# One MLP block instead of two halves, sample rows in column strips, and smaller mask and scratch tiles in the recurrence

## The reference, cut to what matters

```python
# recurrence, per head (64 x 64 state S), six heads
sa = einsum('nhij,nhj->nhi', S, -kk_t)
S = S * w_t + sa * (kk_t * a_t) + v_t * k_t        # outer products
y_t = einsum('nhij,nhj->nhi', S, r_t)
# afterwards group norm of y per head, bonus term, gate

u = einsum('nld,df->nlf', rmsnorm(x, norm2_g), mlp_up)          # 1024 -> 4096
x = x + einsum('nlf,fd->nld', square(relu(u)), mlp_down)        # 4096 -> 1024
y = rmsnorm(x, final_norm_g)
```

## Time and profile before

| | |
|---|---|
| median of three runs | 3599.7 us (3597.3 to 3603.0) |
| the profiled execution | 3601.9 us |
| its span, first to last instruction | 3600.1 us |
| mean granted TensorE clock | 0.927 |
| TensorE busy in matmuls | 3212.1 us |
| VectorE, ScalarE, GpSimd busy | 1604.0, 828.3, 345.7 us |
| recurrence cp, about | 1046 to 1720 us of the span |
| recurrence cs, about | 1720 to 1830 us |
| MLP half ma, first to last matmul | 2065.6 to 2783.6 us |
| MLP half mb, first to last matmul | 2803.7 to 3592.9 us |

### The profile page before, as it was taken

The page is one execution under the profiler, slowest core; times in us unless marked ns, Lnnn a source line. Parts: engine busy times, 40 slices in busy tenths (PEclk is TensorE's granted clock), DMA queues, the critical chain, the costliest instruction groups (busy, mean ns, idle before and its releaser), DMA issues. The chain is left out here.

```text
span 3600.1 us, 65975 instructions
## 1 busy us (share of the span) xinstructions
PE 3212.1 (89%) x27206; PEld 2722.0 (76%) x27206; DVE 1604.0 (45%) x3139; ACT 828.3 (23%) x1540; POOL 345.7 (10%) x473
## 2 busy tenths in 40 slices
PE   7999998997957788878479789999998799999998
PEld 7999985564646677777458578888887688888887
DVE  6111113764125556554233344444445444444445
ACT  5000002653002222221122221212112222111122
POOL 3000002641002322321000000000000000000000
PEclk9999999998658989999579899999999899999999
DMA  4212213323310000000145531111111411111011
GB/s 148 69 69 70 71 71 109 119 67 122 153 62 18 23 23 23 23 23 11 28 150 175 177 115 47 47 47 47 47 47 56 164 48 47 47 47 35 35 47 60
DMA packets 142775, 250.57 MB, mean 70 GB/s; under 512 B 20785, under 2 KB 100977, under 8 KB 139737
## 3 DMA queue, kind: packets, MB, share of 16 engines
q1 hardware_dynamic: 142552, 247.37, 20.4%
HBM read 186.81 MB, written 60.52 MB: 69 GB/s over the span
## 5 line engine op out<-in xcount | busy, mean ns | idle before, releaser
L185 PE MATMUL p_bank<-p_xh,p_wh 128*128 128x416 f32 x800 | 286.0, 357 | 11.6 <-DVE p_wl L306 11.6
L186 PE MATMUL p_bank<-p_xl,p_wh 128*128 128x416 f32 x800 | 283.5, 354 | 0.0
L187 PE MATMUL p_bank<-p_xh,p_wl 128*128 128x416 f32 x800 | 282.4, 353 | 0.0
L2362 DVE TENSOR_TENSOR mb_y<-mb_y,mb_db 128x512 f32<-128x512 f32 (+1 forms) x288 | 197.4, 686 | 185.0 <-PE mb_db L2223 184.4
L2221 PE MATMUL mb_ub<-mb_hh,mb_wuh 128*128 128x352 f32 x768 | 251.4, 327 | 29.0 <-DVE mb_hl L2324 21.7
L2222 PE MATMUL mb_ub<-mb_hl,mb_wuh 128*128 128x352 f32 x768 | 248.6, 324 | 0.0
L2223 PE MATMUL mb_ub<-mb_hh,mb_wul 128*128 128x352 f32 x768 | 248.4, 323 | 0.0
L2362 DVE TENSOR_TENSOR ma_y<-ma_y,ma_db 128x512 f32<-128x512 f32 x256 | 175.8, 687 | 149.7 <-PE ma_db L2223 148.9
L2221 PE MATMUL mb_db<-mb_wdh,mb_uh 128*128 128x512 f32 (+1 forms) x576 | 228.1, 396 | 3.6 <-issue 3.6
L2223 PE MATMUL mb_db<-mb_wdh,mb_ul 128*128 128x512 f32 (+1 forms) x576 | 226.9, 394 | 0.0
L2222 PE MATMUL mb_db<-mb_wdl,mb_uh 128*128 128x512 f32 (+1 forms) x576 | 226.9, 394 | 0.0
(11 more groups left out here) (415 smaller groups left out, 6549.0 us busy)
## 6 DMA issues: line engine op xcount, KB each, us to landing
out_projT<-p_ob SPq DMA_DIRECT2D x100, 208.0 KB, 1.9
ma_wur<-w_up SPq DMA_DIRECT2D x32, 512.0 KB, 6.0
ma_wdr<-w_dn SPq DMA_DIRECT2D x32, 512.0 KB, 4.4
mb_wur<-w_up SPq DMA_DIRECT2D x32, 512.0 KB, 5.8
mb_wdr<-w_dn SPq DMA_DIRECT2D x32, 512.0 KB, 4.2
cp_z<-out_projT SPq DMA_DIRECT2D x8, 1408.0 KB, 7.0
p_kc<-kbT SPq DMA_DIRECT2D x8, 1344.0 KB, 5.9
p_vc<-vb SPq DMA_DIRECT2D x8, 1344.0 KB, 8.7
```

The lines of the kernel that those rows point to most:

```text
L185: pe.matmul(out, wh_, mh, start=(k == 0), stop=False)
L186: pe.matmul(out, wh_, ml, start=False, stop=False)
L187: return pe.matmul(out, wl_, mh, start=False, stop=(k == KC - 1))
L2362: dve.tensor_tensor(ys, ys, db[b % ND][0:n, :], ALU.add).then_inc(y_added, 1)
```

## The change

Both MLP halves become one block, `mlp`, with one set of tiles. `Half` holds where a half's blocks, units and turns start to count. TensorE's order at the seam is now `up(first,15)`, `down(first,14)`, `up(second,0)`, `down(first,15)`, `up(second,1)`, `down(second,0)`. h2T goes through three buffers `hr` of its own. All tiles of h, hidden columns included, are 1056 wide for both halves. The 32 sample rows leave the row tiles of the second half: a float32 product with raw down weights puts block j and output half h into 32-row strip 2h + j of a bank `tb`; VectorE adds the bank to `yt`, and two products with `pick` add up the strips at the very end. The first half's final norm is done in one go inside the second half's super 0, its stores and the reload of y follow. In the recurrence the masks are kept once and read with a repeat, `d`, `cp` and `tC` go (zs, lw and tB take their place), the three banks `pb` become one tile of two banks, so that four groups of three vector instructions and one of three activations become one each, and `hback` is padded with zeros to 96 contracted rows.

```diff
-        mAB = s.sb(n_("mAB"), [P, NP3, 2, C])
-        mL = s.sb(n_("mL"), [P, len(levels), U, C])
+        mAB = s.sb(n_("mAB"), [P, 2, C])
+        mL = s.sb(n_("mL"), [P, len(levels), C])
-        hback = s.sb(n_("hback"), [96, P])
+        hback = s.sb(n_("hback"), [96, NP3, P])
-        pb = [s.ps(n_(f"pb{i}"), [P, 512]) for i in range(3)]
+        pbanks = s.ps(n_("pb"), [P, 4, 256])
+        pb = pbanks[:, 0:NP3, 0:W]
+        many = lambda ap, n: ap.unsqueeze(1).broadcast_to([ap.shape[0], n, *ap.shape[1:]])
...
-                        mm = e.matmul(pb[p][:, 0:W], hback[32 * p:32 * p + 32, :], ksum[32 * p:32 * p + 32, :],
+                        mm = e.matmul(pb[:, p, :], hback[:, p, :], ksum[:, :],
...
-                    for p in range(NP3):
-                        i_ = e.tensor_tensor(kk[:, p, :], kk[:, p, :], pb[p][:, 0:W], ALU.mult)
-                    V.done(i_, "kkn", seg)
+                    V.done(e.tensor_tensor(kk[:, :, :], kk[:, :, :], pb[:, :, :], ALU.mult), "kkn", seg)
...
-                    G.done(e.tensor_tensor(d[:, :, :].rearrange("p z (b q) -> p z b q", b=nb) if sample else d[:, :, :],
+                    W_(E, "a_pre", seg - 2); W_(S, "sgate", seg - 2); W_(E, ("tok", ngr - 1, 2), seg - 2)
+                    W_(V, "bv", seg - 2)
+                    zs = zs_[seg % NPAR]
+                    G.done(e.tensor_tensor(zs[:, :, :].rearrange("p z (b q) -> p z b q", b=nb) if sample else zs[:, :, :],
...
+            def load_h(H, k):
+                n = H.index * KC + k
+                if n >= NR:
+                    sp.wait_ge(h_low, n - NR + 1)
+                w = width(H)
+                sp.dma_start(hr[n % NR][:, 0:w], h2T[k, :, H.c0:H.c0 + w]).then_inc(h_in[n % NR], 16)
...
+            def load_down(n, m, j, tail=None):
+                sp.wait_ge(wd_low, n - 1)
+                if tail is not None:
+                    sp.wait_ge(down_done, turns(second, tail) + 1)
+                sp.dma_start(wdr[:, j], w_dn[m]).then_inc(wd_in[j], 16)
...
+            load_h(first, 0)
             sp.dma_start(wur[:, 1], w_up[1]).then_inc(wu_in[1], 16)
+            for k in range(1, NR):
+                load_h(first, k)
+            for k in range(NR, KC):
+                load_h(first, k)
...
+            for k in range(NR):
+                load_h(second, k)
+            for j in range(2):
+                load_up(FFB + j, j, j)
+            for k in range(NR, KC):
+                load_h(second, k)
+            for j in range(2):
+                load_down(FFB + j, j, j)
+            for j in range(2):
+                load_up(FFB + 2 + j, 2 + j, j)
+            for a in range(NT):
+                sp.wait_ge(normed, a + 1)
+                sp.dma_start(y_out[P * a:P * a + P, :], y[:, a, :]).then_inc(out_st[a], 16)
+            for a in range(NT):
+                sp.wait_ge(out_st[a], 16)
+                sp.dma_start(y[:, a, :], x2[second.c0 + P * a:second.c0 + P * a + P, :]).then_inc(y_in, 16)
+            load_up(FFB + 4, 4, 0)
+            for j in range(2):
+                load_down(FFB + 2 + j, 2 + j, j, 0)
+            with sp.Fori(1, FFB // 2 - 2) as i:
+                load_up(FFB + 2 * i + 3, 2 * i + 3, 1)
+                load_up(FFB + 2 * i + 4, 2 * i + 4, 0)
+                for j in range(2):
+                    load_down(FFB + 2 * i + j + 2, 2 * i + j + 2, j, i)
...
+                if H.tail:
+                    if not start:
+                        pe.wait_ge(y_added, t0 - per(H) + 1)
+                    pe.wait_ge(u_tail, (sup + 1) * SUP)
+                    for j in range(SUP):
+                        pe.wait_ge(wd_in[j], (H.block0 // SUP + sup + 1) * 16)
+                    for h in range(2):
+                        for j in range(SUP):
+                            q = 2 * h + j
+                            mm = pe.matmul(tb[NS * q:NS * (q + 1), :], ut[:, par, j, :], wdr[:, j, h * 512:(h + 1) * 512],
+                                           start=True, stop=True, tile_position=(0, NS * q))
+                    mm.then_inc(down_done, 1)
+                pe.wait_ge(u_low, units(H, sup, SUP))
...
+                            if b == 0:
+                                pe.wait_ge(wd_low, blocks(H, sup, j) + 1)
...
+                    up(H, sup, start)
+                    if not start:
+                        down(H, sup - 1, 1 - par, isinstance(sup, int) and sup == 1)
+                    elif H.index:
+                        down(first, NSUP - 1, (NSUP - 1) % 2, False)
...
+                    high_u(first, sup, 1, 1, False)
+                    for k in range(KC):
+                        high_h(second, k)
+                    act.wait_ge(down_done, turns(first, sup))
...
-            dve.wait_ge(fg_in, 16)
+                    if H.tail and g == ng - 1:
+                        rt = r[:, q, n - NS:n]
+                        dve.tensor_tensor(ut[:, par, j, :], rt, rt, ALU.mult).then_inc(u_tail, 1)
...
+            def finish_first():
+                add_down(first, NSUP - 1, False)
+                dve.wait_ge(fg_in, 32)
+                dve.wait_ge(rooted, 1)
+                dve.reciprocal(st[:, 2, 0:NT], st[:, 1, 0:NT]).then_inc(inverted, 1)
+                dve.wait_ge(inverted, 1)
+                for a in range(NT):
+                    dve.scalar_tensor_tensor(out=y[:, a, :], in0=y[:, a, :], scalar=st[:, 2, a:a + 1], in1=fgb[:, :],
+                                             op0=ALU.mult, op1=ALU.mult).then_inc(normed, 1)
...
+                    if start and H.index:
+                        finish_first()
+                    if not start:
+                        each = (lambda a: low_h(second, a)) if last and H.index == 0 else None
+                        add_down(H, sup - 1, isinstance(sup, int) and sup == 1, each)
+                    low_down(H, sup)
```

More of the change, by code:

```diff
@@ L1 @@
+from collections import namedtuple
 from contextlib import ExitStack
@@ L2220, in passes @@
+            sp.wait_ge(tail_st, 16)
+            for a in range(NT):
+                sp.wait_ge(out_st[a], 32)
         def passes(pe, out, wh, wl, mh, ml, first, last):
@@ L2238, in up, with collect @@
                         mm.then_inc(up_done, 1)
-            def down(sup, par, first):
-                pe.wait_ge(u_low, (sup + 1) * SUP * ng)
-                pe.wait_ge(wd_low, (sup + 1) * SUP)
-                for a, (t0, n) in enumerate(tiles):
+            def collect():
+                pe.wait_ge(y_added, turns(second, NSUP - 1) + 1)
+                pe.wait_ge(relued, units(second, NSUP))
+                pe.wait_ge(fg_in, 32)
+                for h in range(2):
+                    mm = pe.matmul(ub[h][0:NS, :], pick[:, h, :], yt[:, :], start=True, stop=True)
+                mm.then_inc(tail_done, 1)
@@ new lines, in down @@
+            def down(H, sup, par, start, end=False):
+                t0 = turns(H, sup)
+                if H.tail:
[4 more added lines that the diff above has]
+                        pe.wait_ge(wd_in[j], (H.block0 // SUP + sup + 1) * 16)
+                    for h in range(2):
+                        for j in range(SUP):
[4 more added lines that the diff above has]
+                pe.wait_ge(u_low, units(H, sup, SUP))
+                for a in range(NT):
@@ new lines, in _, with body @@
+            for H in halves:
+                def body(sup, par=None):
+                    start = par is None and sup == 0
+                    par = sup % 2 if par is None else par
+                    up(H, sup, start)
[3 more added lines that the diff above has]
+                        down(first, NSUP - 1, (NSUP - 1) % 2, False)
+                super_loop(pe, body)
+            down(second, NSUP - 1, (NSUP - 1) % 2, False, True)
@@ new lines, in square, with stats_first @@
+            def square(a, n):
+                m = rows(a)
+                if n:
+                    act.wait_ge(squared, n)
+                act.activation(hr[0][0:m, 0:D], ys(a)[0:m], ACT.Square, accum_out=st[0:m, 0, a:a + 1]).then_inc(squared, 1)
+            def stats_first():
+                act.wait_ge(eps_set, 1)
+                for a in range(NT):
+                    act.wait_ge(y_added, turns(first, NSUP - 1) + 2 * a + 2)
+                    square(a, a)
+                act.wait_ge(squared, NT)
+                act.activation(st[:, 1, 0:NT], st[:, 0, 0:NT], ACT.Sqrt, bias=eps[:, 0:1], scale=1.0 / D).then_inc(rooted, 1)
@@ new lines, in _ @@
+            super_loop(act, body_first)
+            high_up(second, 0, 1, units(first, NSUP))
+            super_loop(act, body_of(second))
+            for n, a in enumerate(finals):
+                m = rows(a)
+                if a == NT:
+                    act.wait_ge(tail_out, 1)
+                else:
+                    act.wait_ge(y_added, turns(second, NSUP - 1) + 1 + 2 * a + 2)
+                act.wait_ge(inverted, 1)
+                square(a, NT + n)
+                act.wait_ge(squared, NT + n + 1)
```

(26 more changed lines are left out.)

427 lines of the change are left out of this document (232 added, 195 removed).

## The result

The changed kernel took **3543.0 us** (median of four runs, 3539.5 to 3545.9) beside 3598.5 for the kernel before in the same rounds: ratio **0.9845**, 95% interval 0.9828 to 0.9862. The forecast was 3538 in 3514 to 3570. The profiled execution took 3545.9, its span is 3543.8. Of all executions shown here one, in `norm_later`, fell in the slow state (4826.9 us at a mean granted clock of 0.607, where the others of that kernel had 0.93 to 0.94), and its ratio is taken without it.

The account below looks back on a forecast made before the run. TensorE's own work was taken to decide, plus the seams where it idles. 32.6 + 11 + 28.0 - 1.4 - 10 + 2 = 62.2 us off the profiled 3601.9, less 2.2 to the median: 3538 us, range 3514 to 3570.

Parts of the forecast that it names:

- Seam: Between the MLP halves: 40.6 us of idling and lower clock go, 8.0 stay; gain 32.6 us, bounds 20 and 40.6.
- the allowance of 1.6 for the tie in splitting h: Seam, up(second,0): VectorE's 2.7 us per tile ties with TensorE's 2.7, so 1.6 us of loss is allowed.
- Start: Start of the first MLP half: the fg wait and the clock loss behind it go; gain 11 us, bounds 6 and 12.
- I charge 1: Start of the first half: h chunks 3 to 7, loaded only as buffers come free, cost 1 us.
- Strips: Sample rows, second half: four products run together in 1.05 us, saving 1.75 a super; gain 28.0 us over 16.
- The rival of serial strips: Second half's sample rows: strips run one after another, 42.9 us worse, 3581 us; chance 0.12.
- the slower rival: Second half's downs: 32-column strips lower the granted clock; at 10 us a super 80 are lost, 3618 us; chance 0.05.
- End: Kernel's end: pick products, one more scaling and a full-tile store, less 2.1 us in the old gap; loss 1.4 us.
- Layout: First half: 1056-wide tiles slow 512-column products, downs by 8.0 us, ups by 2; loss 10 us, bounds 0 and 16.
- The rival that layout costs nothing: Both MLP halves: all downs step at 0.228 us, 10 and 8 us better, 3520 us; chance 0.13.
- Recurrence: Recurrence: smaller masks gain 4 us, padding loses 3.4, merges gain 1.4; gain 2, bounds minus 12 and plus 7.
- Merged instructions save little: Recurrence: merging groups of three instructions saves 0 to 3 us in all, taken as 1.4.

Follow-up runs that it names:

- norm_later: Kernel after, with VectorE splitting the second half's first down and next up weights ahead of the eight normalisations of the first half's rows: ratio 0.9854.
- same_offset: Kernel after with h chunks at once, norms later, next up load earlier, uh, ul and first-half h rows 1024 wide, 32 unused values ahead of y: 3514.8 us.
- u_1024: Kernel after, with uh and ul 1024 columns wide instead of 1056, h not touched: 3528.7 us, ratio 0.9812.

## Why the prediction was right, point by point

- **Seam, 32.6 forecast.** The stretch gained 21.3 with a slower spacing in it: 1344 up and 1536 down products by 0.0053 are 15.4 us lost, so the seam itself gained 36.7 (34.7 if I take the shortest of the four traces of this stretch before). Kept were 4.3 of stall and 1.7 of lower clock, 6.0 instead of 8.0: the allowance of 1.6 for the tie in splitting h was not needed. More had also been lost before than the 40.6 counted. Behind the wait of 3.6 us the kernel before was granted 0.66 of the clock over 5 us, which cost 1.7 and was not in the sum:

```profile
2760.00:2765.00 5.00, 5.00 (x15) 3.98 (x16) 1.08 (x2) 0.00 (x0) 0.00 (x0) 0.66 0.00 0
```

- **Start, 11 forecast, 2.5 measured (2 to 6 by the other traces).** The step that failed is "I charge 1" for the chunks one by one. The wait of 9.9 for fg did go, and the first up product came 3.8 us sooner behind the projection (19.5 instead of 23.3). But from it to the first down product passed 60.8 us, where it had been 59.6. The sum had the chunks 2 us apart; they came 2.7 apart, and the waits for them were 7.8 us, not 1. And the clock behind and between them was 0.80 instead of 0.87: the sum left it out for these waits, though the row for the clock behind a wait stood in the same paragraph. Loading at once gives back 5.3 of each and takes 3.1 for the later first product.
- **Strips, 28.0 forecast, 24.8 by 16 x 1.55.** Concurrency as forecast. The shortfall of 0.20 us a super is the way in and out, 0.08 and 0.11, which the sum named but did not count. The strips themselves were 0.05 cheaper than forecast and the twelve products that went 0.02 cheaper; 0.03 stay open. The Trainium skill (TensorEngine Tiling, Tiling Modes, Key Properties) says that changing the mode drains the engine. The trace shows a delay each way, over 16 supers 3.0 us instead of the 5 estimated from that rule, but no full drain: by their modelled ends the products on either side still overlap the strips by 0.07 or 0.08 us. The rival of serial strips is excluded by 1.00 us for all eight instructions, and the slower rival by the granted clock: 1.00 in the second half from the first strip on.

```profile
2833.00:3527.00 694.00, 692.39 (x3655) 606.92 (x3648) 345.70 (x533) 146.83 (x247) 0.00 (x0) 1.00 0.12 44
```

- **End, loss 1.4 forecast.** Of the second half's 22.3, fifteen supers by 1.55 make 23.3, so that the last super and the end together lose 1.0; with the last super's own 1.55 taken out, the end's loss is 2.6. The wait for the last weight split went from 3.6 to 1.5, as forecast; which of the small terms behind the last addition is too small was not followed up.
- **Layout, loss 10 forecast, 15.4 in this stretch.** The cause named, "width or the offsets that follow from it", was the right pair, and the offsets are what the runs point to: rows of 1024 alone did nothing for the up products, rows of 1024 at the offset of the weights brought the old spacing back. The term was too small because the up products were given 2 of their possible 8. The rival that layout costs nothing fell, and with it the reading of the Trainium skill (TensorE: Matmul & The Clock Gate, Back-to-back issue gap) by which the spacing follows from the number of columns: here 192 products of one size took 43.84 or 44.9 us.
- **Recurrence, gain 2 forecast, 11.9 measured.** Masks +3.3 for +4 and shift 0 for 0 were right. Padding was -6.7 for -3.4 with the sample recurrence, -5.0 in this stretch: right in place, half in size. The step that failed is "Merged instructions save little ... I take 1.4": they brought 13.9. Their direct saving, 0.4 us in a steady segment, fits the 0 to 3 us of the forecast; what was missing is that TensorE's granted clock in the recurrence is not full, and moves with small changes.

The total was near because the recurrence's +9.9 and the seam's +4.1 stood against -8.5 at the start, -5.4 in the layout, -3.2 in the strips and some small ones. The mechanisms of the MLP were the likeliest ones named, but that the forecast is within 5 us owes much to errors that cancel.

## What to carry to other kernels

Where the granted clock is below 1.00 in a stretch, price a change there at both levels. Waits of 0.9 to 3.2 us between chunks cost as much again through the clock, and savings that look trivial (0.12 us a merge) moved more time through the clock than by themselves. When tiles are shared or widened, work out where each operand of the long matmul loops begins, and compare the spacing of equal products before and after. Before trusting a difference of 2 us in a stretch, look at the same stretch in a second trace. And before moving work away from a stall, follow the chain behind it to its last transfer: here the next stall was already as long.

## What the runs showed that I had not expected

- Products of 512 columns start 0.2267 to 0.2270 us apart in stretches where all fixed and moving operands begin at the same offset (first half before, `same_offset`, down products of `u_1024`), and 0.2318 to 0.2333 where they don't: 44.83 to 45.02 us instead of 43.84 for 192. 128 bytes of unused space gave 9.0 us back. The same offset here means the same but for 512 bytes: every fixed operand is 512 bytes long, so every second one begins 512 bytes further, and in `same_offset` the up products of even and odd chunks both start 0.2267 apart. The effect belongs to the stretch and not to a single product: in the kernel after the rows of chunks 3 and 7 do begin at the offset of their weights, by the same measure, and their up products start 0.2317 apart, hardly sooner than the rest (0.2321 to 0.2328). Why it is so, and which differences below 512 are bad, is open. Products of 352 columns did not show it (0.159 in all kernels).
- Five merged instructions a segment raised the granted clock of the recurrence from 0.90 to 0.92 and shortened it by 13.9 us, 5 at most of it directly.
- Two changes of tile shape around the strips cost 0.19 us together (0.08 in, 0.11 out).
